# Retention and the S5 branch's GLU as one stage: sixteen tiles, each with a half strip between its scores and its outputs

## The chip, the cores and the metric

One core of a Trainium2 chip runs the whole program. The metric is the device time of one execution in microseconds (us). Every product runs on TensorE (PE) in fp32; VectorE is DVE, ScalarE is ACT, GpSimd is POOL, and SyncE (SP) issues DMAs.

## What is computed

The reference is one step of a two-layer decoder trunk (2048 prompt tokens and 8 sample tokens, width 1024). The change lies in the first layer, between its input projection and S5 scan, which leave z and y5 in DRAM, and its output projection. `step` runs over 16 blocks of 128 tokens with 4 heads (keys of 128, values of 256); `glu_w` is 1024 x 1024:

```python
    def step(s, inp):
        qb, kb, vb = inp
        scores = jnp.einsum('bhld,bhmd->bhlm', qb, kb) * decay_mask
        o = (jnp.einsum('bhlm,bhme->bhle', scores, vb)
             + jnp.einsum('bhld,bhde->bhle', qb * q_decay, s))
        s = blk_decay * s + jnp.einsum('bhld,bhle->bhde', kb * k_decay, vb)
        return s, o
...
    o_ret, s_ret_new = retention(q, k, v, s_ret.astype(f32))
    a_out = head_group_norm(o_ret, gn_w).astype(h.dtype) * jax.nn.silu(g_a)
...
    y5 = jax.nn.gelu(y5).astype(h.dtype)
    y5 = y5 * jax.nn.sigmoid(y5 @ glu_w + glu_b)
    b_out = y5 * jax.nn.silu(g_b)
    out = jnp.concatenate([a_out, b_out], axis=-1) @ w_out
```

## The kernel before

The program is a row of stages, each between barriers of all engines: `project_s5`, `retention`, `project` under the tag "pg" (the GLU), `combine`, `project_hgrn`. Each stage has one instruction stream per engine, written by hand; semaphores say who waits for whom.

`retention` (tiles named rt_...) runs 16 tiles of 128 tokens through `tile_steps`: a step takes the front half of tile t+1 and the back half of tile t. On PE a step is `turn_v` (8 transposes of the next tile's values, L1634), `turn_k` (4 transposes of rotated keys, L1640), 4 score products (L1665), `turn_o` (8 transposes of the outputs of the tile before, L1646), the outputs (4 x two products, L1675 and L1676) and the new state (4 products, L1682). `turn_v` first waits until the state of the tile before has been taken (`state_done`), because `ps_v` and `ps_s` are the same two PSUM banks 6 and 7; `ps_ot` has banks 2 and 3 for itself. On DVE a step ends with the moments of the outputs (L1549, L1554), the new state (L1594), and then the group norm (L1559, L1562), for which ACT takes a square root (L1512). ACT also copies the values out of PSUM and applies the SiLU gate; POOL rotates queries and keys. The 8 sample tokens follow after the loop, each with its own state.

`project` for the GLU holds y5 as two fp32r parts, h_hi and h_lo, for all 2056 columns. Its prelude loads the 8 rows of y5, rounds each on ACT (L271) and subtracts on DVE (L346). Each of 8 strips of `glu_w` is split on POOL into w_hi and w_lo. A strip is 5 blocks of 408 or 416 columns (`BLOCKS`), a block 8 x 3 products (L384) into one of eight banks; ACT takes the sigmoid (L302), DVE multiplies (L360 to L368). The first strip goes row by row with the prelude.

Of the kernel before, what the change touches and what calls it, by code (L numbers as in the profile page):

```python
# [30 lines left out]
P = 128  # L31
# [8 lines left out]
BLOCKS = [(b, c0, min(TT, (TT // 8 * (b + 1) + 4) // 5 * 8) - c0)  # L40
          for b, c0 in enumerate((TT // 8 * b + 4) // 5 * 8 for b in range(5))]
NB = len(BLOCKS)
# [44 lines left out]
def tile_steps(eng, step):  # L87


    step((0, 0, 0), None)  # L90
    step((1, 0, 1), (0, 0, 0))
    with eng.Fori(0, NT // 2 - 1) as i:
        step((i * 2 + 2, i + 1, 0), (i * 2 + 1, i, 1))
        step((i * 2 + 3, i + 1, 1), (i * 2 + 2, i + 1, 0))
    step(None, (NT - 1, NT // 2 - 1, 1))


# [11 lines left out]


def project(nc, tag, prelude, src, weights, n_strips, dst, consts, glu=None):

    with ExitStack() as ctx:
        def sb(name, shape, dt=F32):
            return ctx.enter_context(nc.sbuf_tensor(f"{tag}_{name}", shape, dt))

        sem = ctx.enter_context(semaphores(nc, tag))

        norm = prelude == "norm"
        h_hi = sb("h_hi", [P, KD, TT], F32R)
        h_lo = sb("h_lo", [P, KD, TT], F32R)
        w_raw = [sb(f"w_raw{i}", [P, KD, P]) for i in range(2)]
        w_hi = [sb(f"w_hi{i}", [P, KD, P], F32R) for i in range(2)]
        w_lo = [sb(f"w_lo{i}", [P, KD, P], F32R) for i in range(2)]
        if norm:
            xt = [sb(f"xt{i}", [P, D]) for i in range(2)]  # L130
            xn = [sb(f"xn{i}", [P, D]) for i in range(2)]
            ident = sb("ident", [P, P])
            wrow = sb("wrow", [P, D])
            stat = [sb(f"stat{i}", [P, 3]) for i in range(2)]
            eps = sb("eps", [P, 1])
        out_flat = [sb(f"out{i}", [P, 2 * L8 * YCH])[:] for i in range(2)]
        if glu:
            bias = sb("bias", [P, KD])
            gate = [sb(f"gate{i}", [P, 2 * L8 * YCH]) for i in range(2)]
            sig = [sb(f"sig{i}", [P, BLK]) for i in range(2)]  # L140
        psum = ctx.enter_context(nc.psum_tensor(f"{tag}_psum", [P, 8, BLK], F32))

        const_ld = sem("const_ld")
        x_ld = [sem(f"x_ld{i}") for i in range(4)]
        w_ld = [sem(f"w_ld{i}") for i in range(2)]
        g_ld = [sem(f"g_ld{i}") for i in range(2)]
        stored = [sem(f"stored{i}") for i in range(2)]
        sq_done, rms_done, rstd_done, eps_set = sem("sq_done"), sem("rms_done"), sem("rstd_done"), sem("eps_set")
        xn_done, tp_done, hi_done, lo_done = sem("xn_done"), sem("tp_done"), sem("hi_done"), sem("lo_done")
        w_hi_done, w_lo_done = sem("w_hi_done"), sem("w_lo_done")  # L150
        blk_done, ev_done = sem("blk_done"), sem("ev_done")
        gate_done, y_done, yg_done = sem("gate_done"), sem("y_done"), sem("yg_done")
        waited = sem("waited")

        def x_tile(t, n):
            return src["x"][t, :, :] if n == P else src["s"]

        def bank_of(b):
            return (4 + b) % 8

        def tp_view(par, n):
            return psum[:, 2 * par:2 * par + 2, :].rearrange("p b (k c) -> p (b k) c", c=P)[:, :, 0:n]

        def staged(k):

            return out_flat[k % 2] if k % 4 < 2 else gate[k % 2][:]

        def y_views(k):

            stage = staged(k).rearrange("p (h t c) -> p h t c", h=2, c=YCH)  # L170
            return [((hf * HALF, (hf + 1) * HALF, L8), stage[:, hf, :, 0:CHH].rearrange("p t c -> p c t"))
                    for hf in range(2)] + \
                [((T, TT, 1), stage[:, 0, 0:1, CHH + 1:YCH].rearrange("p t c -> p c t"))]

        block = ctx.enter_context(nc.Block())

        @block.sync
        def _(sp):
            for par in range(2):
                sp.dma_start(w_raw[par][:], weights[par]).then_inc(w_ld[par], 16)  # L180
            if norm:
                sp.dma_start(wrow[:], src["w"].unsqueeze(0).broadcast_to([P, D])).then_inc(const_ld, 16)
                sp.dma_start(ident[:], consts["ident"]).then_inc(const_ld, 16)
            if glu:
                sp.dma_start(bias[:], glu["bias"]).then_inc(const_ld, 16)

            def load_x(t, use, par, n):
                sp.wait_ge(xn_done, t + 1)
                sp.dma_start(xt[par][0:n, :], x_tile(t, n)).then_inc(x_ld[par], 16)

            if norm:
                with sp.Fori(0, NT // 2) as i:
                    for par in range(2):
                        load_x(i * 2 + par, i, par, P)
                load_x(NT, NT // 2, 0, NS)
            else:
                for k in range(KD):
                    if k >= 4:
                        sp.wait_ge(lo_done, k - 3)
                    sp.dma_start(staged(k).rearrange("p (h n) -> p h n", h=2), src["y"][k]).then_inc(x_ld[k % 4], 16)  # L200

            def raw_strip(i, par):
                sp.wait_ge(w_lo_done, i * 2 + (par + 3))
                sp.dma_start(w_raw[par][:], weights[i * 2 + (par + 2)]).then_inc(w_ld[par], 16)

            def gate_strip(i, par):
                if glu:
                    sp.wait_ge(yg_done, (i * 2 + par) * NB + NB)
                    sp.dma_start(gate[par][:, 0:T].rearrange("p (t c) -> p t c", c=P),
                                 glu["z"][:, :, bass.ds(i * 2 + (par + glu["gate0"]), 1), :]  # L210
                                 .rearrange("t p s c -> p t (s c)")).then_inc(g_ld[par], 16)
                    sp.dma_start(gate[par][:, T:TT],
                                 glu["zs"][:, bass.ds(i * 2 + (par + glu["gate0"]), 1), :]
                                 .rearrange("p s c -> p (s c)")).then_inc(g_ld[par], 16)

            if glu:
                sp.wait_ge(lo_done, KD)
            with sp.Fori(0, n_strips // 2 - 1) as i:
                for par in range(2):
                    gate_strip(i, par)  # L220
                    raw_strip(i, par)
            for par in range(2):
                gate_strip(n_strips // 2 - 1, par)
        @block.gpsimd
        def _(pool):

            pool.sem_inc(w_lo_done, 2)
            with pool.Fori(0, n_strips // 2) as i:
                for par in range(2):
                    pool.wait_ge(w_ld[par], i * 16 + 16)  # L230

                    pool.wait_ge(blk_done, i * (2 * NB) + (par + 1) * NB)
                    pool.sem_inc(waited, 1)
                    pool.tensor_copy(w_hi[par][:], w_raw[par][:]).then_inc(w_hi_done, 1)
                    pool.wait_ge(w_hi_done, i * 2 + (par + 1))
                    pool.tensor_tensor(w_lo[par][:], w_raw[par][:], w_hi[par][:].bitcast(F32),
                                       ALU.subtract).then_inc(w_lo_done, 1)

        @block.scalar
        def _(act):  # L240
            for par in range(2):
                act.sem_inc(stored[par], CREDIT)
            if not glu:
                act.sem_inc(ev_done, NB)

            def square(t, i, par, n=P):
                act.wait_ge(x_ld[par], i * 16 + 16)
                act.wait_ge(tp_done, t + 1)

                act.activation(xn[par][0:n, :], xt[par][0:n, :], ACT.Square, scale=D ** -0.5,  # L250
                               accum_out=stat[par][0:n, 0:1]).then_inc(sq_done, 1)
                act.wait_ge(sq_done, t + 1)
                act.activation(stat[par][0:n, 1:2], stat[par][0:n, 0:1], ACT.Sqrt, bias=eps[0:n, :])\
                    .then_inc(rms_done, 1)

            def high(t, i, par, n=P):
                act.wait_ge(tp_done, t + 3)
                cols = slice(T, TT) if n < P else bass.ds(i * (2 * P) + par * P, P)
# [1095 lines left out]
def retention(nc, a, z, mix, out_p, out_s):  # L1354

    gammas = [1.0 - 2.0 ** (-5.0 - h) for h in range(RH)]
    with ExitStack() as ctx:
# [174 lines left out]
        def _(dve):  # L1532
# [40 lines left out]
            def step(front, back):  # L1573
# [14 lines left out]
                if front:  # L1588
                    turn(*front, P)
# [1178 lines left out]
```

## Time and profile before

| | us |
|---|---|
| median of 3 runs | 3382.51 (3380.43 to 3383.86) |
| the profiled execution | 3387.03 |
| its span from first to last instruction | 3385.3 |
| PE busy | 3110.3 (92%) |
| DVE, ACT, POOL busy | 1449.5, 1025.9, 1048.5 |

The span is the time from the first to the last instruction of the profiled execution. A busy share is a mean over stages with different limits, so the stages that the change touches have to be read by themselves: retention has its first matmul at 1144.96 us, its loop ends near 1328.7 us, the sample tokens follow until the GLU's first DMA at 1387.80 us, and the first DMA of `combine` is at 1614.89 us.

### The profile page before, as it was taken

How to read it: one execution, taken by the hardware profiler on the slowest of the kernel's cores; microseconds unless marked ns; L12 is line 12 of the kernel's file. 1: busy time of each engine (PE TensorE's matmuls, PEld its weight loads, DVE VectorE, ACT ScalarE, POOL GpSimd, SP SyncE). 2: the span in 40 equal slices, each digit the busy share in tenths (PEclk: the TensorE clock that was granted, in tenths of full speed). 3: DMA queues.
4: the chain of work that ended last, by engine and by line, in shares of the span. 5: the costliest groups of instructions: out<-in, count | busy, mean ns of one | idle time of the engine just before them, and what ended most of it. 6: DMA issues, size and time to landing. Idle time of an engine off the chain costs nothing. (4 is left out here: it accounts for less than half of the span.)

```text
span 3385.3 us, 46397 instructions
## 1 busy us (share of the span) xinstructions
PE 3110.3 (92%) x16972; PEld 2739.4 (81%) x16972; DVE 1449.5 (43%) x2909; ACT 1025.9 (30%) x1726; POOL 1048.5 (31%) x662
## 2 busy tenths in 40 slices
PE   6999999799999787689699978999979999997899
PEld 6999899688888576489588858999978888886786
DVE  7999345214420397544300004124345544446442
ACT  4111122312211242433200002025445344355651
POOL 2223222132223374010211211335425344345442
PEclk8999999899999898799899998999979998998899
DMA  5444655455543563442522213333334333333333
GB/s 132 101 125 128 191 169 159 109 132 168 166 126 93 183 211 124 167 128 85 211 81 93 99 60 100 94 119 116 110 104 147 96 126 125 105 124 115 128 122 110
DMA packets 372318, 430.06 MB, mean 127 GB/s; under 512 B 45488, under 2 KB 314416, under 8 KB 362976
## 3 DMA queue, kind: packets, MB, share of 16 engines
q1 hardware_dynamic: 258448, 360.43, 34.0%
q10 hardware_dynamic: 113744, 67.91, 6.7%
q8 instruction: 84, 1.38, 0.2%
q14 instruction: 42, 0.34, 0.0%
HBM read 281.07 MB, written 151.39 MB: 128 GB/s over the span
## 5 line engine op out<-in xcount | busy, mean ns | idle before, releaser
L1114 PE MATMUL p_psum<-p_h_hi,p_w_hi 128*128 128x344 f32 (+1 forms) x1600 | 567.4, 355 | 0.0
L1114 PE MATMUL p_psum<-p_h_hi,p_w_lo 128*128 128x344 f32 (+1 forms) x1600 | 561.1, 351 | 0.0
L1114 PE MATMUL p_psum<-p_h_lo,p_w_hi 128*128 128x344 f32 (+1 forms) x1600 | 559.9, 350 | 0.0
L2506 PE MATMUL p_psum<-p_h_hi,p_w_hi 128*128 128x344 f32 (+1 forms) x1280 | 466.9, 365 | 0.0
L2506 PE MATMUL p_psum<-p_h_lo,p_w_hi 128*128 128x344 f32 (+1 forms) x1280 | 459.9, 359 | 0.0
L2506 PE MATMUL p_psum<-p_h_hi,p_w_lo 128*128 128x344 f32 (+1 forms) x1280 | 459.5, 359 | 0.0
L698 POOL CAST p_w_hi<-p_w_raw 128x1024 fp32r<-128x1024 f32 x80 | 89.6, 1120 | 818.7 <-PE p_psum L1114 673.9
L1114 PEld LDWEIGHTS p_psum<-p_h_hi,p_w_hi 128*128 128x128 f32 x1600 | 302.0, 189 | 36.6 <-issue 9.5
L1114 PEld LDWEIGHTS p_psum<-p_h_hi,p_w_lo 128*128 128x128 f32 x1600 | 302.1, 189 | 29.1
L1114 PEld LDWEIGHTS p_psum<-p_h_lo,p_w_hi 128*128 128x128 f32 x1600 | 302.1, 189 | 28.4
L2266 DVE COPY p_out<-p_psum 128x344 f32<-128x344 f32 (+1 forms) x160 | 93.6, 586 | 492.6 <-PE p_psum L2506 492.5
L2506 PEld LDWEIGHTS p_psum<-p_h_hi,p_w_hi 128*128 128x128 f32 x1280 | 250.9, 196 | 24.1 <-issue 0.2
L2506 PEld LDWEIGHTS p_psum<-p_h_hi,p_w_lo 128*128 128x128 f32 x1280 | 249.3, 195 | 25.3
L2506 PEld LDWEIGHTS p_psum<-p_h_lo,p_w_hi 128*128 128x128 f32 x1280 | 250.1, 195 | 23.8
L746 ACT ACTIVATE p_out<-p_psum 128x344 f32<-128x344 f32 (+1 forms) x160 | 82.2, 514 | 576.0 <-PE p_psum L1114 572.0
L2022 POOL CAST p_w_hi<-p_w_raw 128x1024 fp32r<-128x1024 f32 x64 | 66.8, 1045 | 494.5 <-PE p_psum L2506 440.4
L700 POOL TENSOR_TENSOR p_w_lo<-p_w_raw,p_w_hi 128x1024 fp32r<-128x1024 f32 x80 | 194.7, 2434 | 6.4
L1276 PE MATMUL c_psum<-c_wo_hi,c_m_hi 128*128 128x512 f32 (+1 forms) x480 | 187.6, 391 | 5.4 <-POOL c_m_lo L1249 5.4
L1276 PE MATMUL c_psum<-c_wo_lo,c_m_hi 128*128 128x512 f32 (+1 forms) x480 | 187.3, 390 | 0.0
L1276 PE MATMUL c_psum<-c_wo_hi,c_m_lo 128*128 128x512 f32 (+1 forms) x480 | 187.2, 390 | 0.0
L1249 POOL TENSOR_TENSOR c_m_lo<-c_m_raw,c_m_hi 128x2048 fp32r<-128x2048 f32 (+1 forms) x17 | 74.8, 4402 | 328.7 <-ACT c_m_hi L1324 271.6
L1038 DVE TENSOR_TENSOR p_shared<-p_psum,p_turn_re 128x512 f32<-128x512 f32 x32 | 22.1, 692 | 351.1 <-PE p_psum L1126 351.1
(330 smaller groups left out, 5919.8 us busy)
## 6 DMA issues: line engine op xcount, KB each, us to landing
p_w_raw<-in_w_in SPq DMA_DIRECT2D x144, 512.0 KB, 4.9
z<-p_out ACTq DMA_DIRECT2D x64, 512.0 KB, 3.6
z<-p_out SPq DMA_DIRECT2D x64, 512.0 KB, 3.2
p_raw<-z SPq DMA_DIRECT2D x32, 1024.0 KB, 5.5
rt_raw<-z SPq DMA_DIRECT2D x16, 1536.0 KB, 6.9
c_m_raw<-m SPq DMA_DIRECT2D x16, 1024.0 KB, 7.0
p_xt<-x SPq DMA_DIRECT2D x32, 512.0 KB, 3.8
u_s<-p_out SPq DMA_DIRECT2D x128, 73.0 KB, 3.3
```

What stands on the lines that cost most here:

```text
L698: pool.tensor_copy(w_hi[par][:], w_raw[par][:]).then_inc(w_hi_done, 1)
L700: pool.tensor_tensor(w_lo[par][:], w_raw[par][:], w_hi[par][:].bitcast(F32), ALU.subtract).then_inc(w_lo_done, 1)
L746: act.activation(out_flat[par][:, c0:c0 + n], bank[:, 0:n], ACT.Copy).then_inc(ev_done, 1)
L1038: step(dve.tensor_tensor(m_re[:, :, :, 1:XC], got[:, :, :, NS + 1:IN], re[:, :, :, 1:XC], ALU.mult))
L1114: ins = pe.matmul(bank, wv[par][:, k, :], h[:, k, c0:c0 + n], start=(k == 0 and j == 0), stop=(k == KD - 1 and j == 2))
L1249: pool.tensor_tensor(m_lo[par][:, :, 0:n], m_raw[par][:, :, 0:n], m_hi[par][:, :, 0:n].bitcast(F32), ALU.subtract).then_inc(m_lo_done, 1)
L1276: ins = pe.matmul(psum[0:n, par, half, :], m[par][:, k, 0:n], w[:, k, cols], start=(k == 0 and j == 0), stop=(k == n_k - 1 and j == 2))
L2022: pool.tensor_copy(w_hi[par][:], w_raw[par][:]).then_inc(w_hi_done, 1)
L2266: dve.tensor_copy(out_buf[par][:, c0:c0 + n], ps[:, b, 0:n])\
L2506: ins = pe.matmul(bank, wv[par][:, k, :], h[:, k, c0:c0 + n], start=(k == 0 and j == 0), stop=(k == KD - 1 and j == 2))
```

## The change

`project`, `tile_steps`, `BLOCKS` and `retention` go; `retention_glu` (tiles named rg_...) takes their place. It goes through 16 tiles, fully unrolled, k = 1 to 16, and pairs each with one half strip g = k-1: the first eight are the eight strips of `glu_w` over the first 1024 prompt tokens and the 8 sample tokens (three blocks of 344 columns), the last eight the same strips over the second 1024 tokens (two blocks of 512). h_hi and h_lo hold one half at a time, so rows of y5 are rounded and subtracted ahead of strip 0 and again ahead of strip 8; those two strips take two blocks row by row (`first_blocks`). Each strip of `glu_w` is loaded and split twice. PSUM is laid out anew: `ps_v`, `ps_ot` and `ps_s` share banks 2 and 3, and strip blocks alternate between banks 6 and 7.

```diff
-        ps_ot = ps[:, 2:4, :].rearrange("p b (s c) -> p (b s) c", c=P)
-        ps_v = ps[:, 6:8, :].rearrange("p b (s c) -> p (b s) c", c=P)
-        ps_s = ps[:, 6:8, :].rearrange("p b (s c) -> p (b s) c", c=2 * P)
+        ps_v = ps_ot = ps[:, 2:4, :].rearrange("p b (s c) -> p (b s) c", c=P)
+        ps_s = ps[:, 2:4, :].rearrange("p b (s c) -> p (b s) c", c=2 * P)
...
+        def bank_of(g, b):
+            return 6 + block_no(g, b) % 2
...
         @block.sync
...
+            for k in range(1, NT + 1):
+                g = strip_of(k)
+                if g >= 1:
+                    store_strip(g - 1)
+                    if g + 1 < N_G:
+                        load_gate(g + 1)
+                        load_strip(g + 1)
+                if k + 1 < NT:
+                    raw_free(k - 1)
+                    load(k + 1)
+                if k >= 2:
+                    store(k - 2)
...
         @block.gpsimd
...
+            for k in range(1, NT + 1):
+                g = strip_of(k)
+                if k < NT:
+                    cosines(k, P)
+                gates(k - 1, P)
+                if g + 1 < N_G:
+                    split(g + 1)
+                if k < NT:
+                    rotate(k, P)
...
         @block.scalar
...
+            for k in range(1, NT + 1):
+                g = strip_of(k)
+                if k < NT:
+                    take_v(k, P)
+                if g == KD:
+                    act.wait_ge(blk_done, block_no(KD, 0))
+                    for r in range(KD):
+                        high(1, r)
+                if g % KD:
+                    sigmoid(g, 0)
+                if k < NT:
+                    silu(k, P)
+                if g + 1 < N_G:
+                    strip_gate(g + 1)
+                if g % KD == 0:
+                    sigmoid(g, 0)
+                sigmoid(g, 1)
+                if half_of(g) == 0:
+                    sigmoid(g, 2)
+                deviation(k - 1, P)
...
         @block.vector
...
-                moments(t, par, P)
                 dve.wait_ge(st_mm, t + 1)
-                for h in range(RH):
-                    ins = dve.scalar_tensor_tensor(out=state[:, h, :], in0=state[:, h, :],
-                                                   scalar=gammas[h] ** P, in1=ps_s[:, h, :],
-                                                   op0=ALU.mult, op1=ALU.add)
                 ins.then_inc(state_done, 1)
-                norm_o(t, par, P)
+                moments(k - 1, P)
+                norm_o(k - 1, P)
+                take_state(k - 1)
+                if (g + 1) % KD:
+                    pre(g + 1)
...
         @block.tensor
...
+            def first_blocks(g):
+
+                pe.wait_ge(w_lo_done, g + 1)
+                for b in range(2):
+                    bank_free(g, b)
+                for r in range(KD):
+                    pe.wait_ge(y_lo_done, KD * half_of(g) + r + 1)
+                    for b in range(2):
+                        ins = products(g, b, r)
...
+            for k in range(1, NT + 1):
+                g = strip_of(k)
+                if k < NT:
+                    pe.wait_ge(v_done, k)
+                    pe.wait_ge(state_done, k)
+                    turn_v(k, P)
+                turn_k(k - 1, P)
+                scores(k - 1)
+                if k >= 2:
+                    pe.wait_ge(v_done, min(k + 1, NT))
+                    pe.wait_ge(state_done, k)
+                    turn_o(k - 2, P)
+                if g % KD:
+                    strip_block(g, 0)
+                    strip_block(g, 1)
+                else:
+                    first_blocks(g)
+                if half_of(g) == 0:
+                    strip_block(g, 2)
+                outputs(k - 1)
+                new_states(k - 1)
...
-    retention(nc, a, z0, m0, o["ret_p"], o["ret_s"])
-    project(nc, "pg", "y5", {"y": y5.rearrange("h (k p) l c -> k p h (l c)", p=P)}, a["glu_w"], KD,
-            {"z": m0["z"], "zs": m0["zs"], "first": KD}, consts,
-            glu={"bias": a["glu_b"], "z": z0["z"], "zs": z0["zs"], "gate0": 24})
+    retention_glu(nc, a, z0, y5, m0, o["ret_p"], o["ret_s"])
```

The sample part makes the expanded keys of one head at a time in two buffers, where it made those of all four heads first.

On PE, at the border of two tiles, these stand in a row before (rt_raw is the next tile's input, rt_rot its rotated queries and keys, rt_o_nat the normalised outputs):

```order
L1682 MATMUL rt_psum<-rt_v_nat,rt_k_nat 128x256 x4
L1634 MATMUL rt_psum<-rt_ident,rt_raw 128x128 x8
L1640 MATMUL rt_psum<-rt_ident,rt_rot 128x128 x4
L1665 MATMUL rt_psum<-rt_rot 128x128 x4
L1646 MATMUL rt_psum<-rt_ident,rt_o_nat 128x128 x8
L1675 MATMUL rt_psum<-rt_v_nat,rt_score 128x256
L1676 MATMUL rt_psum<-rt_state,rt_q_dec 128x256
```

And these stand there after the change, in the first token half (rg_h_hi and rg_w_hi are the parts of y5 and of the strip):

```order
L1554 MATMUL rg_psum<-rg_v_nat,rg_k_nat 128x256 x4
L1508 MATMUL rg_psum<-rg_ident,rg_raw 128x128 x8
L1516 MATMUL rg_psum<-rg_ident,rg_rot 128x128 x4
L1524 MATMUL rg_psum<-rg_rot 128x128 x4
L1530 MATMUL rg_psum<-rg_ident,rg_o_nat 128x128 x8
L1561 MATMUL rg_psum<-rg_h_hi,rg_w_hi 128x344
L1561 MATMUL rg_psum<-rg_h_lo,rg_w_hi 128x344
L1561 MATMUL rg_psum<-rg_h_hi,rg_w_lo 128x344
```

The order around the border is the same; the strip's products have come in behind `turn_o`, ahead of the outputs.

On DVE, one step of the loop before, from the decayed keys to the norm:

```order
L1579 TENSOR_TENSOR rt_k_nat<-rt_psum,rt_k_decay 128x512
L1582 TENSOR_TENSOR rt_score<-rt_psum,rt_mask 128x512
L1570 TENSOR_TENSOR rt_mixed<-rt_psum,rt_gate 128x1024
L1543 TENSOR_TENSOR rt_cross<-rt_raw,rt_rope 64x1024 x2
L1549 BN_STATS rt_stats<-rt_psum 128x6 x4
L1554 BN_AGGR rt_mv<-rt_stats 128x2 x4
L1594 SCALAR_TENSOR_TENSOR rt_state<-rt_state,rt_psum 128x256 x4
L1559 RECIPROCAL rt_rstd<-rt_std 128x4
L1562 TENSOR_SCALAR rt_o_nat<-rt_psum,rt_mv,rt_rstd 128x256 x4
```

The same step after the change, from the masked scores on, in the second token half (rg_zg is the strip's gate, rg_out its result):

```order
L1427 TENSOR_TENSOR rg_score<-rg_psum,rg_mask 128x512
L1386 TENSOR_TENSOR rg_gate<-rg_psum,rg_gate 128x1024
L1417 TENSOR_TENSOR rg_out<-rg_out,rg_zg 128x512
L1356 TENSOR_TENSOR rg_cross<-rg_raw,rg_rope 64x1024 x2
L1417 TENSOR_TENSOR rg_out<-rg_out,rg_zg 128x512
L1363 BN_STATS rg_stats<-rg_psum 128x6 x4
L1367 BN_AGGR rg_mv<-rg_stats 128x2 x4
L1373 RECIPROCAL rg_rstd<-rg_std 128x4
L1378 TENSOR_SCALAR rg_o_nat<-rg_psum,rg_mv,rg_rstd 128x256 x4
L1432 SCALAR_TENSOR_TENSOR rg_state<-rg_state,rg_psum 128x256 x4
L1406 TENSOR_TENSOR rg_out<-rg_h_hi,rg_h_lo 128x1024
L1410 TENSOR_TENSOR rg_zg<-rg_zg,rg_out 128x1024
```

The state (L1594, now L1432) has moved from ahead of the reciprocal and the norm to behind them.

## Rows read from the trace of the kernel before

**Rows 1.** Windows view: stretch, us, busy PE PEld DVE ACT POOL, PEclk, DMA, GB/s.

```profile
1145.00:1328.70 183.70, 147.07 (x824) 127.57 (x824) 162.58 (x351) 76.44 (x78) 126.02 (x65) 0.94 0.59 202
1328.70:1387.80 59.10, 44.55 (x156) 24.63 (x156) 22.46 (x39) 4.13 (x5) 0.86 (x2) 0.73 0.23 90
1387.80:1614.90 227.10, 186.18 (x960) 182.80 (x960) 104.61 (x144) 92.39 (x88) 28.56 (x16) 0.92 0.42 133
```

**Rows 2.** Timeline, products of 344 and 512 columns in project_s5: start, us, line.

```profile
299.83 0.32 PE L1114 MATMUL p_psum<-p_h_lo,p_w_hi 128*128 128x344 f32 x1
...
302.99 0.32 PE L1114 MATMUL p_psum<-p_h_hi,p_w_hi 128*128 128x344 f32 x1
...
1099.68 0.40 PE L1114 MATMUL p_psum<-p_h_hi,p_w_hi 128*128 128x512 f32 x1
...
1100.84 0.39 PE L1114 MATMUL p_psum<-p_h_hi,p_w_lo 128*128 128x512 f32 x1
```

**Rows 3.** Waits view, PE in the retention loop: us, times, longest.

```profile
PE rt_psum L1634 <- issue: 13.4, 7, 2.1
PE rt_psum L1634 <- DVE rt_state L1594: 13.2, 7, 1.9
```

**Rows 4.** Timeline of PE around one tile border; idle before in brackets.

```profile
1302.29 1.89 PE L1682 MATMUL rt_psum<-rt_v_nat,rt_k_nat 128*128 128x256 f32 x8
1306.04 1.06 PE L1634 MATMUL rt_psum<-rt_ident,rt_raw 128*128 128x128 f32 x8 [1.86 <-issue]
...
1309.26 0.67 PE L1675 MATMUL rt_psum<-rt_v_nat,rt_score 128*128 128x256 f32 x2
...
1312.79 1.89 PE L1682 MATMUL rt_psum<-rt_v_nat,rt_k_nat 128*128 128x256 f32 x8
```

**Rows 5.** Timeline of DVE and ACT around the same border.

```profile
1302.68 1.43 DVE L1549 BATCH_NORM_STATS2 rt_stats<-rt_psum 128x6 f32<-128x256 f32 x4
1304.26 0.38 DVE L1554 BATCH_NORM_AGGREGATE rt_mv<-rt_stats 128x2 f32<-128x6 f32 x4 [0.15 <-DVE rt_stats L1549]
1304.56 1.38 DVE L1594 SCALAR_TENSOR_TENSOR rt_state<-rt_state,rt_psum 128x256 f32<-128x256 f32 x4
1304.67 0.30 ACT L1512 ACTIVATE rt_std<-rt_mv,rt_eps 128x4 f32<-128x4 f32 x1 [3.34 <-DVE rt_mv L1554]
1305.85 0.17 DVE L1559 RECIPROCAL rt_rstd<-rt_std 128x4 f32<-128x4 f32 x1
1306.06 1.90 DVE L1562 TENSOR_SCALAR rt_o_nat<-rt_psum,rt_mv,rt_rstd 128x256 f32<-128x256 f32 x4
```

**Rows 6.** Waits view, PE in the GLU stage.

```profile
PE pg_psum L384 <- DVE pg_h_lo L346: 25.7, 6, 20.2
PE pg_psum L384 <- DVE pg_out L368: 10.9, 1, 10.9
```

**Rows 7.** Lines view of the GLU's prelude: count, then busy us, mean ns.

```profile
L271 ACT ACTIVATE pg_h_hi<-pg_gate 128x1024 fp32r<-128x1024 f32 x8 | 16.7, 2140 | 0.0
```

**Rows 8.** Timeline of PE: first transposes behind longer waits (idle before in brackets).

```profile
1165.73 1.09 PE L1634 MATMUL rt_psum<-rt_ident,rt_raw 128*128 128x128 f32 x8 [1.81 <-DVE rt_state L1594]
...
1328.72 1.97 PE L1646 MATMUL rt_psum<-rt_ident,rt_o_nat 128*128 128x128 f32 x8 [3.65 <-DVE rt_o_nat L1562]
...
3157.69 0.63 PE L2514 MATMUL p_psum<-p_ident,p_k_dec 128*128 128x128 f32 x4 [3.90 <-DVE p_state L2312]
...
130.87 0.69 PE L1159 MATMUL p_psum<-p_ident,p_shared 128*128 128x128 f32 x2 [4.18 <-DVE p_w_apart L995]
...
3207.03 1.08 PE L2514 MATMUL p_psum<-p_ident,p_k_dec 128*128 128x128 f32 x4 [5.14 <-DVE p_state L2312]
```

**Rows 9.** Windows view of PE alone: stretch, its us, PE busy, PEclk, DMA, GB/s.

```profile
1144.90:1161.00 16.10, 12.06 (x41) 0.50 0.46 170
1328.70:1331.70 3.00, 2.98 (x14) 0.50 0.00 0
1331.70:1334.50 2.80, 1.22 (x8) 0.93 0.62 249
```

More of the change, by code:

```diff
@@ L1407, in retention @@
-        N_CONST = 6
+        gn_w, eye8, eps, bias = sb("gn_w", [P, KD]), sb("eye8", [P, NS, NS]), sb("eps", [P, 1]), sb("bias", [P, KD])
+        raw, rope = two("raw", [P, 24, P]), two("rope", [P, 2, P])
+        rot, gate = two("rot", [P, 8, P]), two("gate", [P, 8, P])
+        q_dec, k_nat, v_nat = two("q_dec", [P, RH, P]), two("k_nat", [P, RH, P]), two("v_nat", [P, RH, 2 * P])
+        cross, score, o_nat, state = (sb("cross", [P, 8, P]), sb("score", [P, RH, P]), sb("o_nat", [P, RH, 2 * P]),
+                                      sb("state", [P, RH, 2 * P]))
@@ new lines, in retention_glu @@
+        k_own = out[0:NS].rearrange("p s c -> p (s c)")[:, 0:2 * NS * P].rearrange("p (s n c) -> p s n c", s=2, c=P)
+        const_ld, bias_ld = sem("const_ld"), sem("bias_ld")
+        ld, stored, w_ld, z_ld, g_stored = ([sem(f"{n}{i}") for i in range(2)] for n in (
+            "ld", "stored", "w_ld", "z_ld", "g_stored"))
+        y_ld = [sem(f"y_ld{i}") for i in range(4)]
+        s_ld, s_stored, p_stored, s_read = [sem(f"s_ld{h}") for h in range(RH)], sem("s_stored"), sem("p_stored"), sem("s_read")
@@ new lines, in strip_of, with store_count, load_count, row_views @@
+        def strip_of(k):
+            return k - 1 if 0 <= k - 1 < N_G else None
+        def store_count(g):
+            return sum(32 if s < KD else 16 for s in range(g % 2, g, 2))
+        def load_count(g):
+            return store_count(g + 2)
+        def row_views(hf, r):
+            stage = staged[:, r % 4, :].rearrange("p (t c) -> p t c", c=YCH)
+            views = [(0, HALF, L8, stage[:, :, 0:CHH].rearrange("p t c -> p c t"))]
+            if hf == 0:
+                views.append((HALF, COLS[0], 1, stage[:, 0:1, CHH + 1:YCH].rearrange("p t c -> p c t")))
+            return views
@@ L1441, in _ @@
[L1441 to L1452 removed]
+            sp.dma_start(bias[:], a["glu_b"]).then_inc(bias_ld, 16)
@@ L1510, in deviation, with silu, strip_gate, sigmoid @@
-            def deviation(t, par, n):
+            def silu(t, n):
+                r = raw[t % 2][:, 16:24, 0:n]
+                act.wait_ge(ld[t % 2], 32 * (t // 2 + 1))
+                act.activation(r, r, ACT.Silu).then_inc(silu_done, 1)
+            def strip_gate(g):
+                v = zg[:, g % 2, 0:COLS[half_of(g)]]
+                act.wait_ge(z_ld[g % 2], load_count(g))
+                act.activation(v, v, ACT.Silu).then_inc(zs_done, 1)
+            def sigmoid(g, b):
+                c0, n = HBLOCKS[half_of(g)][b]
+                act.wait_ge(blk_done, block_no(g, b) + 1)
+                act.wait_ge(pre_done, g + 1)
+                act.activation(out[:, g % 2, c0:c0 + n], ps[:, bank_of(g, b), 0:n], ACT.Sigmoid,
+                               bias=bias[:, g % KD:g % KD + 1]).then_inc(ev_done, 1)
@@ L1511, in deviation @@
+            def deviation(t, n):
+                par = t % 2
                 act.wait_ge(mv_done, t + 1)
                 act.activation(std[par][0:n, :], mv[par][0:n, :, 1], ACT.Sqrt, bias=eps[0:n, :]).then_inc(std_done, 1)
-            def step(front, back):
-                if front:
-                    take_v_and_gate(*front, P)
-                if back:
-                    deviation(back[0], back[2], P)
-            def store_states(act):
-                for h in range(RH):
-                    act.wait_ge(kv_done, (h + 1) * (NS // 2))
-                    act.dma_start(out_s[h], s_state[h][:]).then_inc(s_stored, 16)
@@ L1524, in _, with high @@
[L1524 to L1528 removed]
+            def high(hf, r):
+                act.wait_ge(y_ld[r % 4], 16 * ((KD * hf + r) // 4 + 1))
+                for c0, c1, l, s in row_views(hf, r):
+                    ins = act.activation(h_hi[:, r, c0:c1].rearrange("p (c t) -> p c t", t=l), s, ACT.Copy)
+                    ins.then_inc(y_hi_done, 1)
@@ L1529, in _ @@
+            take_v(NT, NS)
+            silu(NT, NS)
+            for h in range(RH):
+                act.wait_ge(kv_done, (h + 1) * (NS // 2))
+                act.dma_start(out_s[h], s_state[h]).then_inc(s_stored, 16)
+            deviation(NT, NS)
             act.wait_ge(s_stored, 16 * RH)
@@ L1567, in mix_o, with low @@
                 dve.wait_ge(ot_done, t + 1)
                 dve.wait_ge(gate_done, t + 1)
-                dve.wait_ge(stored[par], i * 16 + CREDIT)
-                dve.tensor_tensor(mixed[par][:, :, 0:n], ps_ot[:, :, 0:n], gate[par][:, :, 0:n], ALU.mult)\
+                dve.tensor_tensor(gate[par][:, :, 0:n], ps_ot[:, :, 0:n], gate[par][:, :, 0:n], ALU.mult)\
                     .then_inc(mix_done, 1)
-            def step(front, back):
-                if not back:
-                    turn(*front, P)
-                    return
-                t, i, par = back
+            def low(hf, r):
+                views = row_views(hf, r)
+                dve.wait_ge(y_hi_done, 2 * min(KD * hf + r + 1, KD) + max(0, KD * hf + r + 1 - KD))
+                for c0, c1, l, s in views:
+                    ins = dve.tensor_tensor(h_lo[:, r, c0:c1].rearrange("p (c t) -> p c t", t=l), s,
+                                            h_hi[:, r, c0:c1].bitcast(F32).rearrange("p (c t) -> p c t", t=l),
+                                            ALU.subtract)
+                ins.then_inc(y_lo_done, 1)
@@ L1641, in turn_k, with scores, turn_o @@
                 ins.then_inc(kt_done, 1)
-            def turn_o(t, par, n):
+            def scores(t):
+                if t:
+                    pe.wait_ge(sc_done, t)
+                r = rot[t % 2]
+                for h in range(RH):
+                    ins = pe.matmul(ps_score[:, h, :], r[:, RH + h, :], r[:, h, :], start=True, stop=True)
+                ins.then_inc(sc_mm, 1)
+            def turn_o(t, n):
                 pe.wait_ge(o_done, t + 1)
                 for s in range(8):
-                    ins = pe.transpose(ps_ot[:, s, 0:n], o_nat[par][0:n, s // 2, (s % 2) * P:(s % 2 + 1) * P],
+                    ins = pe.transpose(ps_ot[:, s, 0:n], o_nat[0:n, s // 2, (s % 2) * P:(s % 2 + 1) * P],
@@ L1647, in turn_o, with outputs @@
                                        ident[0:n, 0:n])
                 ins.then_inc(ot_done, 1)
-            def step(front, back):
-                if front:
-                    if back:
-                        pe.wait_ge(v_done, front[0])
-                        pe.wait_ge(state_done, front[0])
-                    turn_v(*front, P)
-                if not back:
-                    return
-                t, _, par = back
-                later = par or not isinstance(t, int)
-                if later:
-                    pe.wait_ge(k_done, t)
-                    pe.wait_ge(sc_done, t)
-                turn_k(t, par, P)
-                for h in range(RH):
-                    ins = pe.matmul(ps_score[:, h * P:(h + 1) * P], rot[par][:, RH + h, :], rot[par][:, h, :],
-                                    start=True, stop=True)
-                ins.then_inc(sc_mm, 1)
-                if later:
-                    turn_o(t - 1, 1 - par, P)
+            def outputs(t):
+                par = t % 2
@@ L1683, in step, with products @@
                 ins.then_inc(st_mm, 1)
-            tile_steps(pe, step)
-            turn_o(NT - 1, 1, P)
+            def products(g, b, r):
+                c0, n = HBLOCKS[half_of(g)][b]
+                par = g % 2
+                for j, (w, h) in enumerate(((w_hi, h_hi), (w_hi, h_lo), (w_lo, h_hi))):
+                    ins = pe.matmul(ps[:, bank_of(g, b), 0:n], w[par][:, r, :], h[:, r, c0:c0 + n],
+                                    start=(r == 0 and j == 0), stop=(r == KD - 1 and j == 2))
+                return ins
```

703 lines of the change are left out of this document (262 added, 441 removed).

## The prediction

> **What bounds the kernel now.** I read the stages first, then each stage's waits, then the timelines at those waits. The stages that the change joins take 183.70 us (retention's loop), 59.10 us (its sample tokens) and 227.10 us (the GLU) [rows 1]. In none of them is PE without a break: it is busy 147.07, 44.55 and 186.18 us. The GLU stage has little to hide: of its 41 us without a product, 25.7 us are the wait for the rows of y5 to be split, 20.2 us of it in one piece ahead of the first product, and 10.9 us are one stall at the second strip [rows 6]. The loop's idle time is another kind: 14 waits of 1.9 us, one at each border of two tiles, half of them put down to the state and half to nothing visible, but of the same length [rows 3]. The chain there reads off two timelines. PE starts the state products at 1302.29 [rows 4]; DVE takes the moments from 1302.68, is through with them at 1304.64, and updates the state until 1305.94 [rows 5]; PE's transposes of the next tile start at 1306.04 [rows 4]. So DVE's moments and state lie on the path, and the reciprocal and the norm, which run until 1307.96, do not.
>
> **The change part by part.** The idea of the pairing is that strips fill the gaps of retention. But the strip stands between `turn_o` and the outputs; the gap is at the border, behind the state products, and nothing has been put into it. So the strip's products come on top of the tile's.
>
> (A) The GLU stage goes: -227.1 us, with its start, its stall, its barrier and its drain [rows 1].
>
> (B) The strips' products come back inside the tiles. Twenty steps of 344 columns took 3.16 us, so 0.158 each, and five of 512 columns 1.16 us, so 0.232 [rows 2]. Eight strips of 3 x 24 products and eight of 2 x 24 make 8 x 72 x 0.158 = 91.0 and 8 x 48 x 0.232 = 89.1, together +180.1 us at full clock.
>
> (C) The border wait grows. DVE now does the reciprocal and the norm before the state. From the start T of the moments (1302.68 in the rows): moments done at T+1.96, square root on ACT 0.30, reciprocal 0.17, with handoffs some 0.57 in all, norm 1.90, state 1.38, so PE may go on at about T+5.88 where it did at T+3.36 [rows 4, 5]. This is +2.52 us at each of 14 borders, 35.3; at the two last places, where PE waited for the norm itself, it is only the difference of the two ends, T+5.88 against T+5.28, about 0.6 each. Sum +36.5 us, and the wait is 1.86 + 2.52 = 4.38 us. Behind the waiting transposes on PE everything of the next tile is queued; ACT's copy of the values waits for them too. The range is narrow, since every operation has a row: 30 to 40.
>
> (D) The start. The first strip's rows pass ACT one by one, 2.14 us each [rows 7]; DVE's subtraction of a row is taken to be as long. If the first row's rounding ends near 1145, when PE starts now [rows 9], eight rows with the tile's own copy and gate between them end near 1165, the last subtraction at 1167. Then come two DVE products over the half strip (at most 2 x 2.14), a sigmoid that frees the bank of the third block (about 1), that block (24 x 0.158 = 3.8), outputs and states (5.4 by rows 4: 3.53 to 1312.79, then 1.89) and the wait (4.4): 1186. The first tile ran at a clock of 0.50 until 1161 [rows 9]; as the products are again row by row with gaps, I add 4: 1190. The second tile starts now at 1165.73 [rows 8]. Of the 24.3 us between, 11.4 (the strip) and 2.5 (the border) stand in B and C; what is left is +10.4, range 5 to 15.
>
> (E) The ninth strip needs the second half of y5, and its rows can't be rounded before the eighth strip has read the first half. ACT starts on them once it has copied the values, 3.1 us into the tile; 8 x 2.14 + 2.14 puts the last subtraction at 22.4, and six products of 0.232 later the two blocks end near 23.8. An ordinary strip would have ended at 3.22 (the front, 1306.04 to 1309.26 [rows 4]) + 11.1 = 14.3. So +9.3, range 6 to 11.
>
> (F) The clock. Behind the loop's waits of 1.8 to 1.9 us the tile's eight transposes take 1.06 to 1.09 us [rows 4, 8]. Behind 3.65 us eight take 1.97, at half speed; behind 4.18 two take 0.69, and behind 5.14 four take 1.08; behind 3.90, four took 0.63, full speed [rows 8]. The granted clock says the same: 0.50 for 3.0 us behind the 3.65 us wait, 0.93 after that [rows 9]. A wait of 4.38 lies among those that mostly cost the clock. With 3.2 us at 1.2 instead of 2.4 GHz, each border gives up 1.6 us: 14 x 1.6 = +22.4, range 0 to 45. I take the middle, as three of the four long waits end that way.
>
> The Trainium skill ("TensorE: Matmul & The Clock Gate", "HAM oscillation — how this bites in real kernels") tells of a kernel whose loop held a wait in every pass and that went back to half clock in every pass; the rows agree for three waits of four, and one row differs. By that rule F would stand as it is, at 22.4; by the one row that differs it would be nothing, the second rival below.
>
> (G) At nothing: the sigmoids, POOL's splits (now 16 strips' worth instead of 8), the doubled weight loads, SP's order and DVE's gate products. A tile will take about 26 us (3.2 + 11.3 + 5.4 + 4.4 + 1.6). DVE has 162.58 + 104.61 us of work for 16 such tiles, some 17 us each, ACT 76.44 + 92.39, some 11, POOL 126.02 and twice 28.56, some 11.5 [rows 1]. SP issues the strip's store and loads ahead of the next raw tile, a whole tile before they are needed, and the loop moved 202 GB/s before against some 140 now. The sample tokens keep their 59.1 us, less a few as three of four key copies leave their start: -3 to +1, taken as 0. If the cover is gone, the price is that of the fourth case below.
>
> Sum: -227.1 + 180.1 + 36.5 + 10.4 + 9.3 + 22.4 = +31.6. On the profiled execution of 3387.0 us this gives 3418.6; that execution is 4.5 us above the median, so 3414 beside the median of 3382.5.
>
> **The rivals.** What a measurement of this kernel can tell from no change is about 0.2%, 6.8 us.
>
> Clock low at each border, as summed: 3414, own range 3398 to 3430.
>
> The clock holds. Place: the border; price: F and the 4 us of half clock in D; point from which it decides: PE, after 11 us of products without a break, restarts at full clock behind 4.4 us, as it did behind 3.90 [rows 8]. Then +31.6 - 22.4 - 4 = +5.2; with the sample part at full clock too (0.73 now [rows 1], some 6 us of its transposes and small products) -0.8: 3382 to 3388, not slower. With D and E at their low ends it would be some 8 us faster still. Against it stand three rows of four.
>
> The low clock lasts. The front of a tile is transposes and four short products, with a wait for the rotated keys in it; at the loop's start the clock stayed at 0.50 for 16 us while PE was 75% busy [rows 9]. If it comes back only in the strip, the whole front (3.22 us) is doubled and some 3.3 us of strip run at half clock: 3.22 + 1.63 = 4.85 per border, 14 x (4.85 - 1.6) = +45.5: 3460. Against it: behind 3.65 us the clock was back after 3 us of transposes [rows 9].
>
> Operands come late. A strip's weights, its gate or its free bank arrives behind PE's need, as at the GLU's second strip (10.9 us once [rows 6]); SP's queue is in order, and POOL splits the strip ahead of the rotation. At a fifth of that per tile, 2.2 x 14 = +31: 3445.
>
> **How the numbers follow.** Clock low at each border 0.52; clock holds 0.22; long low clock 0.12; late operands 0.08; a cheaper start together with a clock that holds 0.06. Likeliest: 3414. Faster by over 0.2% needs the last case and a part of the second: 0.10. Within 0.2% lies most of the second: 0.16. The rest is slower: 0.74. For 8 in 10 the range reaches down through the second case to 3380 and up through late operands to 3450, and leaves out the long low clock and the fastest ends.
>
> **What would show it.** C: DVE's row order norm, then state, and a PE wait of about 4.4 us ahead of `turn_v` at 14 borders. If the waits are 1.9, the step C is wrong. F: granted clock near 0.5 for some 3 us behind each border; eight transposes of about 2 us there. A and B: PE's sum of products in the joint stage near 370 us at full clock, no GLU stage. D and E: the first tile some 45 us from its first transposes, and the ninth some 9 longer than its neighbours. G: no waits of PE for weights or banks inside strips; such waits, or a stage whose pitch is far from 26 us, would make the prediction wrong.

## The result and the profile after

The changed kernel takes 3412.91 us, the median of 4 runs (3409.22 to 3420.08), against 3383.19 us before in the same session: 1.0092 times as long, 95% interval 1.0074 to 1.0110. It is slower by 29.7 us; 31.6 us slower was forecast, 3414 us in all.

Its page has busy times 17 us (PE) to 53 us (POOL) above those before (the engines' totals, busy us, share of the span and instructions):

```profile
span 3408.8 us, 45839 instructions
...
PE 3127.3 (92%) x16972; PEld 2743.0 (80%) x16972; DVE 1476.9 (43%) x2861; ACT 1044.2 (31%) x1748; POOL 1101.1 (32%) x678
```

The windows view cuts each program at the end of `project_s5`'s products and at the first DMA of `combine` (columns as in rows 1). Before, and after:

```profile
1128.45:1614.89 486.44, 377.84 (x1940) 335.07 (x1940) 290.69 (x536) 173.56 (x172) 155.48 (x83) 0.89 0.47 156
...
1131.85:1653.00 521.15, 403.99 (x1940) 347.12 (x1940) 317.19 (x488) 191.91 (x194) 208.20 (x99) 0.84 0.45 154
```

The stretch that the change touches is 34.7 us longer with the same 1940 instructions on PE, which stand for 26 us more busy time at a granted clock of 0.84 instead of 0.89. The code around it is the same in both, and in these two executions it differs by some 11 us the other way, so single terms are read inside this stretch. The stretch after the change by part: start, tiles 2 to 8, tile 9, tiles 10 to 14, the last two tiles with the sample tokens:

```profile
1131.90:1199.00 67.10, 29.34 (x124) 26.11 (x124) 49.86 (x47) 28.98 (x30) 37.95 (x13) 0.66 0.63 219
1199.00:1380.90 181.90, 153.50 (x868) 146.91 (x869) 112.53 (x189) 70.78 (x77) 83.11 (x42) 0.89 0.47 158
1380.90:1418.90 38.00, 25.84 (x100) 20.77 (x100) 32.17 (x35) 24.73 (x17) 11.93 (x6) 0.81 0.61 211
1418.90:1547.80 128.90, 108.64 (x500) 93.21 (x500) 74.34 (x131) 49.19 (x50) 62.89 (x31) 0.90 0.45 150
1547.80:1653.00 105.20, 86.68 (x348) 60.13 (x348) 48.30 (x89) 18.21 (x20) 12.32 (x8) 0.81 0.27 92
```

Ordinary tiles take 181.9 / 7 = 26.0 and 128.9 / 5 = 25.8 us; 26 was forecast. Of PE's waits in the stretch (us, times, longest) the first line answers to [rows 3]; the second is the two last places, where no next tile's values are turned:

```profile
PE rg_psum L1508 <- issue: 60.0, 14, 7.3
PE rg_psum L1530 <- DVE rg_state L1432: 6.7, 2, 4.0
```

Thirteen border waits are 4.05 us and one, behind the ninth tile, is 7.30. One border on PE, DVE and ACT, to be laid beside [rows 4, 5]:

```profile
1245.10 1.89 PE L1554 MATMUL rg_psum<-rg_v_nat,rg_k_nat 128*128 128x256 f32 x8
1251.04 1.94 PE L1508 MATMUL rg_psum<-rg_ident,rg_raw 128*128 128x128 f32 x8 [4.05 <-issue]
...
1245.30 1.43 DVE L1363 BATCH_NORM_STATS2 rg_stats<-rg_psum 128x6 f32<-128x256 f32 x4 [0.61 <-PE rg_psum L1544]
1246.76 0.38 DVE L1367 BATCH_NORM_AGGREGATE rg_mv<-rg_stats 128x2 f32<-128x6 f32 x4
1247.18 0.30 ACT L1303 ACTIVATE rg_std<-rg_mv,rg_eps 128x4 f32<-128x4 f32 x1 [3.48 <-DVE rg_mv L1367]
1247.51 0.18 DVE L1373 RECIPROCAL rg_rstd<-rg_std 128x4 f32<-128x4 f32 x1 [0.36 <-ACT rg_std L1303]
1247.72 1.90 DVE L1378 TENSOR_SCALAR rg_o_nat<-rg_psum,rg_mv,rg_rstd 128x256 f32<-128x256 f32 x4
1249.53 1.41 DVE L1432 SCALAR_TENSOR_TENSOR rg_state<-rg_state,rg_psum 128x256 f32<-128x256 f32 x4
```

The norm stands between the moments and the state; PE goes on 0.1 us behind the state, at T+5.74 from the start of the moments (T+5.88 was forecast), and its eight transposes take 1.94 us, half speed. PE alone in the 8 us behind two borders, and in the strip that follows the first (us, PE busy, PEclk, DMA, GB/s):

```profile
1225.70:1233.70 8.00, 7.97 (x50) 0.81 0.78 309
1277.30:1285.30 8.00, 7.99 (x41) 0.62 0.62 236
1229.00:1236.00 7.00, 7.00 (x51) 1.00 0.47 184
```

The granted clock is half at the front of a tile and full in the strip. A mean of 0.81 over 8 us stands for 3.0 us at half clock, one of 0.62 for 6.1; read in this way, the half clock lasts 2.7 to 3.2 us behind five of the 14 borders and 4.3 to 6.1 behind nine, 4.5 on average.

### The profile page after: what moved, and what is told of

Same layout as the page of the kernel before. It is cut to its first block and busy times, and to the rows that moved or that the text cites. A ratio compares the mean times of both kernels' runs of the same rounds, so it can differ in the third digit from the quotient of the medians.

```text
span 3408.8 us, 45839 instructions
## 1 busy us (share of the span) xinstructions
PE 3127.3 (92%) x16972; PEld 2743.0 (80%) x16972; DVE 1476.9 (43%) x2861; ACT 1044.2 (31%) x1748; POOL 1101.1 (32%) x678
```

## The experiments

e1 to e7 and e9 are edits of the changed kernel, e8 of the kernel before. Each ratio is to the kernel before in the same session; the changed kernel's is 1.0092.

### e1: the state ahead of the norm again

```diff
-                norm_o(k - 1, P)
                 take_state(k - 1)
+                norm_o(k - 1, P)
```

> One edit: on DVE the new state is taken ahead of the norm again, as before the change; PE's order stays. Theory (the border wait is DVE's chain, and its length costs the clock): PE's wait ahead of the next tile's transposes falls from 4.05 us to about 1.9, and the transposes start at full clock (eight in 1.06 us instead of 1.94); 2.15 + 1.93 us at 14 borders, about 57 us less than the changed kernel, near 3356. Rival 1 (the half clock has another cause than the length of the wait): only the wait shrinks, about 30 us less, near 3383. Rival 2 (something else ends as late as the state, for example the norm that turn_o waits for): the wait moves to turn_o, little or no gain, 3400 to 3413.

3355.81 us, 0.9920 (0.9892 to 0.9947): 57 us less than the changed kernel. The border on PE and DVE:

```profile
1236.99 1.89 PE L1554 MATMUL rg_psum<-rg_v_nat,rg_k_nat 128*128 128x256 f32 x8
1240.43 1.06 PE L1508 MATMUL rg_psum<-rg_ident,rg_raw 128*128 128x128 f32 x8 [1.55 <-issue]
...
1238.94 1.38 DVE L1432 SCALAR_TENSOR_TENSOR rg_state<-rg_state,rg_psum 128x256 f32<-128x256 f32 x4
1240.45 1.90 DVE L1378 TENSOR_SCALAR rg_o_nat<-rg_psum,rg_mv,rg_rstd 128x256 f32<-128x256 f32 x4
```

At 13 borders the wait is 1.55 us and the transposes run at full speed; the one behind the ninth tile is still 4.80 us, at half speed. Both rivals fall: the gain is more than the 2.5 us of wait at each border, 35 in all, and nothing else ends as late as the state. With this order, the kernel with the joint stage is 0.8% faster than the kernel before.

### e2: transposes without use inside the wait

```diff
                 new_states(k - 1)
+                if k < NT - 1:
+                    for j in range(20):
+                        pe.transpose(ps_k[:, j % RH, :], ident[:], ident[:])
```

> One addition: behind the state products of each tile PE does 20 transposes of the identity into a bank that is free there, about 2.2 us, inside the border wait; nothing else moves, so the next tile can start no earlier. Theory (the length of PE's idle stretch costs the clock): the idle stretch falls to about 1.9 us, the next tile starts at full clock, and each tile is 1.9 us shorter although more work is done: about 27 us less than the changed kernel, near 3386. Rival (the clock falls for another reason): no gain, 3413, or some us more where the added work delays the tile.

3385.28 us, 1.0005 (0.9992 to 1.0018): 28 us less than the changed kernel, with more work on PE. A border:

```profile
1261.13 1.89 PE L1554 MATMUL rg_psum<-rg_v_nat,rg_k_nat 128*128 128x256 f32 x8
1262.86 2.35 PE L1613 MATMUL rg_psum<-rg_ident 128*128 128x128 f32 x20
1267.07 1.07 PE L1508 MATMUL rg_psum<-rg_ident,rg_raw 128*128 128x128 f32 x8 [1.86 <-issue]
```

From the state products to the next tile it is 5.94 us, the same as in the changed kernel (1251.04 - 1245.10), but PE sits idle for 1.86 of them instead of 4.05, and the next tile starts at full clock. So it is at 13 borders; behind the ninth tile PE still idles for 5.14 us, and the eight transposes take 1.72. The half clock is a cost of its own, some 28 us, apart from the wait, and here it hangs on PE's idle stretch.

### e3: strip blocks inside the border

```diff
+                if g % KD:
+                    turn_k(k - 1, P)
+                    scores(k - 1)
+                    strip_block(g, 0)
                 if k < NT:
                     pe.wait_ge(v_done, k)
                     pe.wait_ge(state_done, k)
                     turn_v(k, P)
+                if g % KD:
+                    strip_block(g, 1)
...
                     turn_o(k - 2, P)
```

> The strip's blocks are spread: turn_k, the scores and the first block stand at the border, ahead of the wait for the state; then turn_v, the second block, turn_o and, in the first half, the third block. The norm stays ahead of the state on DVE, whose rotation products and first gate product move ahead of the mix. Tiles 1 and 9 keep their order. Theory (the wait is bare because the strip does not stand in it): the 4.05 us wait and the 1.93 us of half clock go at 13 borders, about 78 us less, near 3335, with tiles of 20 us. Rival (DVE, ACT or POOL take the place: DVE has some 17 us of work per tile, the rotation comes late): tiles of 22 to 24 us, 3355 to 3385.

3330.39 us, 0.9848 (0.9818 to 0.9878): 82 us less than the changed kernel. Five tiles of the first half and five of the second by windows:

```profile
1219.70:1317.60 97.90, 97.90 (x621) 94.37 (x620) 83.53 (x136) 50.62 (x55) 64.06 (x31) 1.00 0.62 211
1375.00:1472.00 97.00, 97.00 (x501) 82.48 (x500) 81.31 (x132) 49.24 (x50) 65.31 (x32) 1.00 0.58 196
```

PE has no idle time there and the clock is 1.00: tiles of 19.6 and 19.4 us. The norm is still ahead of the state; its place costs nothing once PE has a block to do meanwhile. DVE, busy 83.53 of 97.90 us, does not take the place. One border, the one ahead of tile 9, keeps its 4.05 us.

### e4 and e6: why the ninth tile is 12 us longer than its neighbours

e4 leaves the rounding of the second half out.

> Left out: of the eight rows of y5's second half only 8 columns each are rounded and subtracted, so the GLU of the second half runs on stale values; every wait stays. It prices step E. Theory (the ninth tile is long because the rows pass ACT and DVE one by one ahead of its strip): the ninth tile falls from 38.0 to about 26 us, 12 us less than the changed kernel, near 3401. Rival (the ninth tile is long for another reason, its loads or its first gate): 0 to 5 us less.

3408.21 us, 1.0076 (1.0048 to 1.0105), a miss: some 5 us less, not 12. In its trace the ninth tile runs from 1380.53 to 1411.39, 30.9 us instead of 38.0, so the rounding is 7.1 us of the 12.2 by the trace, while the two totals lie within each other's intervals. The wait behind the tile is there still:

```profile
1411.39 1.94 PE L1510 MATMUL rg_psum<-rg_ident,rg_raw 128*128 128x128 f32 x8 [7.24 <-issue]
```

The changed kernel's DVE at the end of that tile shows what is late:

```profile
1404.86 1.23 DVE L1406 TENSOR_TENSOR rg_out<-rg_h_hi,rg_h_lo 128x1024 f32<-128x1024 f32 x1
1406.12 1.23 DVE L1410 TENSOR_TENSOR rg_zg<-rg_zg,rg_out 128x1024 f32<-128x1024 f32 x1
1407.38 2.45 DVE L1356 TENSOR_TENSOR rg_cross<-rg_raw,rg_rope 64x1024 f32<-64x1024 f32 x2
1409.87 3.44 DVE L1417 TENSOR_TENSOR rg_out<-rg_out,rg_zg 128x512 f32<-128x512 f32 x2
1410.47 2.83 DVE L1417 TENSOR_TENSOR rg_out<-rg_out,rg_zg 128x512 f32<-128x512 f32 x1
1409.98 2.78 POOL L1232 TENSOR_TENSOR rg_rot<-rg_rot,rg_cross 128x1024 f32<-128x1024 f32 x1 [24.07 <-PE rg_psum L1544]
1413.23 1.41 DVE L1363 BATCH_NORM_STATS2 rg_stats<-rg_psum 128x6 f32<-128x256 f32 x4
```

The outputs were done by 1409.9 (the state products start at 1409.77), but the moments stand behind two gate products of the strip until 1413.23. The second of the two (shown once more by itself) takes 2.83 us, where each gate product of this size takes 0.69 in the tiles behind; it runs beside POOL's sum for the rotation and ends 0.55 us behind it. So some 2.1 of the 3.25 us by which this wait is longer are one slow product; no run moved POOL's sum alone. e6 moves these two behind the state in that tile alone:

```diff
-                post(g, 1)
+                if g != KD:
+                    post(g, 1)
...
                 take_state(k - 1)
+                if g == KD:
+                    post(g, 0)
+                    post(g, 1)
```

> One edit on the changed kernel: in the ninth tile DVE does the strip's two gate products behind the state instead of ahead of the moments. It prices the part of step E that the rounding does not explain. Theory (in that tile the moments stand on DVE behind gate products that wait for a late sigmoid, so the border wait behind it is 7.30 instead of 4.05 us): that wait falls to about 4.1, 3.2 us less in all, near 3410. Rival (the outputs of that tile themselves come late): no change, 3413.

3411.14 us, 1.0076 (1.0057 to 1.0094): the time can't tell it from the changed kernel, but the row can, since the wait is 4.05 us:

```profile
1416.31 1.07 PE L1512 MATMUL rg_psum<-rg_ident,rg_raw 128*128 128x128 f32 x8 [4.05 <-issue]
```

The ninth tile takes 35.8 us there, 2.2 less and not 3.25, as its outputs start 1.0 us later. Of the 12.2 us, 7.1 are the rounding and 3.25 this wait; the other 1.9 no run prices.

### e5 and e9: the start

> The start alone is edited, on the changed kernel: SP issues the constants, the rows of y5 and the first strip ahead of the second tile's input; PE does turn_k, the scores and the first strip's two blocks before it turns the second tile's values; DVE makes the first strip's gate product ahead of the first tile's keys and scores. It prices step D, in which the second tile starts at 1199 us where 1190 was forecast. Theory (the rows wait for DMAs that are queued behind other loads, the longest wait of ACT there being 14 us, and then for PE's and DVE's order): the second tile starts 4 to 8 us sooner relative to the end of project_s5, 3405 to 3409 in all. Rival (the eight rows are bound by ACT's and DVE's own work): within 2 us of the changed kernel, 3411 to 3414.

3413.72 us, 1.0077 (1.0057 to 1.0097): no gain that can be measured, as the rival has it. In the trace the second tile starts at 1195.87, 63.8 us after `project_s5`, against 67.2: 3.4 us, short of the 4 to 8 but above the rival's 2. The order of the loads and of the first operations is a small part. e9 leaves the rounding of the first half out:

> Left out: of the eight rows of y5's first half only 16 columns each are rounded and subtracted (the other columns of both parts are set to zero while the engines wait for the first loads), so the GLU of the first half runs on zeros; loads, waits and PE's work stay. It prices the rounding in step D, for which the second tile started 67.2 us after project_s5's last product, where the kernel before needed 36.9. Theory (half of D is the rounding of eight rows on ACT and DVE, the other half loads, the third block's bank and the slow clock): the second tile starts 6 to 10 us sooner after project_s5, near 58 to 61, and the whole takes 3403 to 3407. Rival (D is loads and queues alone): 65 to 67 us, and 3410 to 3413 in all.

3403.38 us, 1.0062 (1.0043 to 1.0081), 9.5 us less than the changed kernel, in the theory's range though the two intervals just overlap. The second tile:

```profile
1188.61 1.94 PE L1514 MATMUL rg_psum<-rg_ident,rg_raw 128*128 128x128 f32 x8 [4.05 <-issue]
```

That is 57.4 us after `project_s5`'s last product (which ends at 1131.26 there), so the rounding is 9.9 us of the start.

### e8: the kernel before with the norm ahead of the state

```diff
+                norm_o(t, par, P)
                 dve.wait_ge(st_mm, t + 1)
...
                 ins.then_inc(state_done, 1)
-                norm_o(t, par, P)
```

> The kernel before, with one edit: in retention's loop DVE does the norm ahead of the state, the order of the changed kernel; no strips, no other change. Theory (that order alone makes the long wait and the half clock, whatever else is in the tile): the border wait goes from 1.9 to about 4.2 us, the transposes behind it run at half clock, each of 14 tiles is 2.3 + 1.9 us longer, about 59 us more than before, near 3443. Rival (the half clock needs the strip's dense products ahead of the wait, or the tile of 10 us absorbs it): only the wait, about 32 us more, near 3416.

3440.39 us, 1.0166 (1.0143 to 1.0189): 54 us more than the kernel before. Its waits, which answer to [rows 3]:

```profile
PE rt_psum L1634 <- DVE rt_state L1595: 31.7, 7, 4.7
PE rt_psum L1634 <- issue: 31.1, 7, 4.6
```

The wait is 4.5 us on average, 36 us more in all than the 1.9 before. The rest goes with the clock, by windows from the second tile on to the loop's end or near it, in this run and in the kernel before (the 0.94 of [rows 1] has the slow first tile in it):

```profile
1166.00:1350.00 184.00, 128.14 (x624) 115.55 (x624) 125.26 (x270) 59.34 (x60) 95.49 (x50) 0.84 0.49 167
...
1166.00:1328.70 162.70, 131.85 (x772) 115.17 (x770) 149.01 (x332) 69.53 (x71) 108.86 (x57) 0.98 0.60 206
```

The rival, the wait alone, falls. So the order on DVE makes the loss by itself, without any strip.

### e7: the edits together

e7 puts e3, e1's order, e5's start and e6's late gates together and rounds two rows of the second half ahead of the ninth tile's values.

> All edits together: strip blocks spread over the border as in the third run, the state ahead of the norm, the start's order and the late gate products, and two rows of the second half rounded ahead of the ninth tile's values. Theory (the terms add): from 3330, some 3 us for the ninth border (4.05 to 1.5 and its half clock), 3 for the late gates, 4 for the two rows and 4 to 8 at the start: 3312 to 3318. Rival (DVE and POOL, which the spread strip has made tighter, take part of it back): 3320 to 3328.

3324.43 us, 0.9816 (0.9795 to 0.9836): 62 us less than the kernel before and the lowest median of all, but only 6 less than e3, where 12 to 18 were expected; by their intervals the two can't be told apart. The rival's range holds it. The ninth tile still takes some 31 us, with waits of 3.30 and 1.94 us for rounded rows, and in the two tiles behind it PE waits for rotated keys:

```profile
1364.57 0.66 PE L1530 MATMUL rg_psum<-rg_ident,rg_rot 128*128 128x128 f32 x4 [0.72 <-POOL rg_rot L1232]
1386.02 0.66 PE L1530 MATMUL rg_psum<-rg_ident,rg_rot 128*128 128x128 f32 x4 [1.81 <-POOL rg_rot L1232]
```

Which of the small edits were taken back there was not tried one by one.

## Why the prediction was right

**Stage against strips (A, B).** The tiles of e3, without any wait, show the strip at its price: 19.6 us, where the front, strip, outputs and states of the forecast sum to 3.2 + 11.4 + 5.4 = 20.0.

**The border (C).** Right in its mechanism, a little too large: 4.05 instead of 4.38 us, so 2.15 us more than before at each of 14 borders (the excess of the ninth tile's stands under E), 30.1 of the 36.5 us. DVE had its earlier work done sooner than in the loop before (the moments start 0.20 us behind the state products' start, before 0.39 [rows 4, 5]), and the chain from there to PE was 0.14 us shorter (5.74 instead of 5.88). e1 and e8 show the mechanism from both sides.

**The clock (F).** Right, and too small: 28 us by e2, 22.4 forecast. The low stretch was put at 3.2 us; it is 4.5 on average, up to 6.1, which at half clock would give up some 31 us over 14 borders. All 14 go to half clock, so the rival that the clock holds was wrong; e6 has the one border that differs (below). The Trainium skill ("TensorE: Matmul & The Clock Gate", "HAM oscillation — how this bites in real kernels") tells of a kernel that waits for a DMA in every pass of its loop and starts every pass at half clock; the trace agrees at all 14 borders of the changed kernel, where the wait is one for DVE.

**The start (D).** The step failed in size, beyond its range: 67.2 us from `project_s5` to the second tile against 37.3 before, less the strip's 11.4 and the border's 2.2, is 16.3 where 10.4 (5 to 15) stood. The term that was mis-sized is DVE's subtraction, which was taken to be as long as ACT's 2.14 us a row. From the end of the first row's rounding to the last subtraction 22 us stood; the trace has 29.9 (1148.6 to 1178.5), and DVE works through 28.95 of them without a break, 3.6 us a row. All sixteen pieces, then the last one beside what POOL does, and a piece of the same size in the kernel before:

```profile
1149.55 28.95 DVE L1393 TENSOR_TENSOR rg_h_lo<-rg_staged,rg_h_hi 128x1024 fp32r<-128x1024 f32 x16
...
1174.41 4.06 POOL L1256 TENSOR_TENSOR rg_w_lo<-rg_w_raw,rg_w_hi 128x1024 fp32r<-128x1024 f32 x1
1176.24 2.26 DVE L1393 TENSOR_TENSOR rg_h_lo<-rg_staged,rg_h_hi 128x8 fp32r<-128x8 f32 x1
...
1433.45 0.17 DVE L346 TENSOR_TENSOR pg_h_lo<-pg_gate,pg_h_hi 128x8 fp32r<-128x8 f32 x1
```

A row's 1024 columns take about the 2.14 us forecast, but the 8 sample columns behind them take 0.94 to 2.32 us in seven rows of eight, 13.1 us in all. In each of the seven this piece ends within 0.03 us of the end of an operation of POOL that ran beside it. In the sixth row, with POOL idle, it takes 0.15 us, and in the kernel before, where POOL's work ended ahead of the rows, 0.15 to 0.20. That POOL holds it up is read from these ends; no run took POOL's work away. From the last subtraction to the second tile it is 20.6 us, where 23 stood, so the rows make the whole excess over the forecast. e9 prices the rounding at 9.9 of the 16.3; e5 got 3.4 back in its trace by order alone.

**The ninth tile (E).** 12.2 instead of 9.3 (by the step's own ends, 23.8 less 14.3, it is 9.5), range 6 to 11, for a cause that the step did not have: with the strip's gate late, DVE's gate products stand ahead of the moments, one of them slow beside POOL, and the border behind is 3.25 us longer. Without that it is 9.0. e4 and e6 part the two.

**At nothing (G).** Right but for DVE's gate products, which cost nothing in an ordinary tile and 3.25 us in the ninth (E): no strip waits for weights or banks in an ordinary tile, and the sample part is a few us shorter.

Together: -227.1 + 180.1 + 14 x 2.15 + 16.3 + 12.2 + 28 = +39.6 against 34.7 in the stretch. 2.9 of the difference is the sample part (from the last transposes of prompt outputs to the next stage 56.2 us instead of 59.1); the other 2 stay open. That the total came so near the forecast is in part luck: D, E and F were 14 us too small together, C 6 too large, and the code around the stretch ran some 11 us faster in the profiled executions.

## What to carry to other kernels

When two stages are joined so that one fills the other's gaps, look where in the order the gap is: work that stands on the other side of it adds to the time and fills nothing. A step that only this tile's output needs (the norm) must not stand ahead of one that the next tile waits for (the state), unless the waiting engine has something to do. And a wait on PE costs more than its length if PE goes on at half clock behind it; here 4.05 us cost some 6, and useless products in it paid. Last, an operation's price from a stretch where the other engines rest (0.15 us for the 8 sample columns) need not hold where they work (up to 2.32).

## What had not been expected of the hardware

Twenty transposes without use made the kernel 28 us faster, as they kept PE's idle stretch at 1.86 us. And the half clock does not follow from the length of the wait alone: in e6 the border behind the ninth tile is 4.05 us like the others, but its eight transposes take 1.07 us, full speed. PE had worked there with gaps of 0.5 to 3.3 us, between rows that came late; what in that decides was not tried.

A subtraction of 128x8 on DVE that takes 0.15 us with POOL idle took up to 2.32 us beside POOL's work, and ended with it (D).
